# Row norms built from accumulated sums, an earlier tile 0 at each boundary, and slope tables on GpSimd, in a two-block transformer stack on one core

## The reference

```python
def first_block(x, ...):
    for i in range(2):
        h = rms_norm(x, norm_pre[i])
        y = gmlp_mixer(h, ...) if i == 0 else dilated_attention_mixer(h, ...)
        x = x + rms_norm(y, norm_post[i])
    return x

def second_block(x, mem, ...):
    for layer in range(2):
        x = layer_norm_2(A * x + 0.5 * swiglu(x, ffn_w_gu[layer, 0], ffn_w_down[layer, 0]), ...)
        o_tok, q_mem = mla_mix(x, ...) if layer == 0 else nsa_mix(x, ..., *shared)
        o_mem = memory_attention(q_mem, mem, w_mem_kv[layer])
        mix = concatenate([o_tok, o_mem]) @ w_out[layer]
        x = layer_norm_2(A * x + mix, ...)
        x = layer_norm_2(A * x + 0.5 * swiglu(x, ffn_w_gu[layer, 1], ffn_w_down[layer, 1]), ...)
        if layer == 0:
            shared = nsa_shared_kv(x, nsa_w_kv, cmp_pos, cmp_w1, cmp_b1, cmp_w2)
    return x
```

## Time and profile before

| | us |
|---|---|
| median of 3 runs | 3189.24 (3189.17 to 3189.56) |
| the profiled execution, its own time | 3191.15 |
| its span | 3189.4 |
| TensorE busy | 3021.9 |
| VectorE busy | 1295.6 |
| ScalarE busy | 1048.1 |
| GpSimd busy | 139.1 |

### The profile page before, as it was taken

How to read it: one execution, slowest core, us unless ns; L and a number is a source line. 1 busy time by engine, 2 the same in 40 slices (tenths; PEclk the granted TensorE clock), 3 DMA queues, 4 the chain that set the end, 5 groups by cost and what they waited for, 6 DMA issues and landing times.

```text
span 3189.4 us, 36596 instructions
## 1 busy us (share of the span) xinstructions
PE 3021.9 (95%) x15462; PEld 2516.9 (79%) x15462; DVE 1295.6 (41%) x1859; ACT 1048.1 (33%) x1808; POOL 139.1 (4%) x214
## 2 busy tenths in 40 slices
PE   8999989999999899999889999899999978999998
PEld 6888878888888788887668888688888854688886
DVE  3463243333326532325654332423332558553224
ACT  3323234443444322213642222113221237522221
POOL 1000010030001000001000000100000100010000
PEclk9999999999999999999999999999999979999999
DMA  5333222232221223223112332432233410122321
GB/s 194 125 102 105 93 93 67 86 94 86 82 77 47 96 90 104 93 95 100 40 40 80 99 99 93 108 106 93 93 96 102 116 40 1 40 80 93 106 93 66
DMA packets 135010, 280.06 MB, mean 88 GB/s; under 512 B 20378, under 2 KB 33098, under 8 KB 134720
## 3 DMA queue, kind: packets, MB, share of 16 engines
q1 hardware_dynamic: 125232, 247.17, 24.1%
q0 software_dynamic: 9616, 30.57, 3.0%
HBM read 271.30 MB, written 4.25 MB: 86 GB/s over the span
## 4 chain that ended last, share of the span: by engine, by line
PE 86%; DVE 8%; ACT 2%; issue 2%; DMA 1%; POOL 1%; SPq 0%; DVEq 0%; POOLq 0%; ACTq 0%
PE bank L528 24%; PE bank L530 24%; PE bank L529 24%; PE bank L681 2%; PE bank L660 2%; PE bank L714 2%; PE bank L539 1%; PE bank L542 1%; PE bank L541 1%; PE bank L733 1%; PE bank L669 1%; PE bank L722 1%; PE bank L641 1%; DVE n_p L1623 1%; DVE x_rows L1554 1%
## 5 line engine op out<-in xcount | busy, mean ns | idle before, releaser
L1492 DVE TENSOR_TENSOR w_low<-raw,w_high 128x2048 fp32r<-128x2048 f32 (+2 forms) x221 | 499.9, 2262 | 1303.4 <-ACT w_high L1135 1297.1
L528 PE MATMUL bank<-xt_high,w_high 128*128 128x512 f32 x1984 | 779.6, 393 | 3.7 <-DVE w_low L1492 3.3
L530 PE MATMUL bank<-xt_high,w_low 128*128 128x512 f32 x1984 | 773.8, 390 | 0.0
L529 PE MATMUL bank<-xt_low,w_high 128*128 128x512 f32 x1984 | 773.2, 390 | 0.0
L1135 ACT ACTIVATE w_high<-raw 128x2048 fp32r<-128x2048 f32 (+2 forms) x221 | 417.5, 1889 | 991.1 <-PE bank L530 991.1
L528 PEld LDWEIGHTS bank<-xt_high,w_high 128*128 128x128 f32 x1984 | 372.5, 188 | 81.3 <-DVE w_low L1492 3.8
L530 PEld LDWEIGHTS bank<-xt_high,w_low 128*128 128x128 f32 x1984 | 372.4, 188 | 79.8
L529 PEld LDWEIGHTS bank<-xt_low,w_high 128*128 128x128 f32 x1984 | 372.7, 188 | 75.8
L528 PE MATMUL bank<-w_high,hidden_high 128*128 128x512 f32 x704 | 277.1, 394 | 3.1 <-DVE gate_rows L1821 3.1
L529 PE MATMUL bank<-w_low,hidden_high 128*128 128x512 f32 x704 | 275.7, 392 | 0.0
L530 PE MATMUL bank<-w_high,hidden_low 128*128 128x512 f32 x704 | 275.4, 391 | 0.0
(11 more groups left out here) (327 smaller groups left out, 3902.8 us busy)
## 6 DMA issues: line engine op xcount, KB each, us to landing
raw<-in_ffn_w_gu SPq DMA_DIRECT2D x80, 1024.0 KB, 5.1
raw<-in_ffn_w_down SPq DMA_DIRECT2D x44, 1024.0 KB, 5.0
raw<-in_b_w_in SPq DMA_DIRECT2D x40, 1024.0 KB, 5.2
raw<-in_a_w_in SPq DMA_DIRECT2D x24, 1024.0 KB, 5.2
raw<-in_a_w_out SPq DMA_DIRECT2D x8, 1024.0 KB, 5.0
raw<-in_ffn_w_gu SPq DMA_DIRECT2D x16, 512.0 KB, 4.4
raw<-in_w_out SPq DMA_DIRECT2D x5, 1024.0 KB, 5.0
raw<-in_w_mem_kv SPq DMA_DIRECT2D x4, 1024.0 KB, 5.2
```

Source lines behind the costliest of these rows:

```text
L528: pe.matmul(o, lh, rh, start=start, stop=False, skip_group_check=True)
L529: pe.matmul(o, lh, rl, start=False, stop=False, skip_group_check=True)
L530: return pe.matmul(o, ll, rh, start=False, stop=stop, skip_group_check=True)
L1492: dve.tensor_tensor(homes[n][1][:, 0:w], RAW[n % 2][:, 0:w], homes[n][0][:, 0:w].bitcast(F32), ALU.subtract).then_inc(sem["w_low_ready"], ...
```

## The change

1. The last blocks of a product ahead of a boundary: tile 0 goes through both last panels first, then tile 1. Turn 0 stands between the two blocks of tile 2, turn 1 between those of tile 3 (before: ahead of them). l02 keeps the old order of the first four blocks.
2. The last panel of the product ahead of a boundary gets a home of its own (not at l02), and the homes of a boundary are free from the fifth last panel on (the fourth last where there are four panels). Both of the next product's first panels are converted ahead of tile 0 (at l02 only the first).
3. A LayerNorm tile: VectorE reads the banks with accumulated sums, makes minus the mean in one small operation, and writes (row - mean) times the gain into x; beside that ScalarE squares the centred row with an accumulated sum. VectorE makes the mean square plus epsilon, GpSimd only the power, and VectorE scales and adds the bias. VectorE waits for GpSimd's power right behind the mean square. s1 and s2 get the same small steps on VectorE, with the power alone on GpSimd. So do s0, the v norm and the MLA norms. The written order of tiles on VectorE is begin 0, end 0, begin 1, low 0, end 1, begin 2, low 1, end 2, begin 3, end 3, low 2, low 3 (`begin` is `center` or `add` below, `end` the last scaling, `low` the low part of the turned tile), with the conversions of the two edge panels in front; ScalarE's is square 0, square 1, split 0, square 2, split 1, square 3, split 2, split 3.
4. GpSimd waits for the second kv_a panel before it issues the seven loads ahead of the roots of l02.
5. The slope tables are made by GpSimd in two operations each. Table 0 follows the nsa_a product, table 1 the read of the compressed outputs, and table i from 2 on the masks of group i-2. VectorE waits for them.
6. VectorE's attention loop: at each odd n one reciprocal of two columns, and the scalings of tasks n-3 and n-2 behind it.

```diff
+    EDGES = {"s1": ("a_out", ("b", 0, 0, "q"), (64, 72, 80, 32), (0, 8)),
+             "s2": ("b_out", ("gate", 0, 0, 0), (0, 8, 24, 32), (48, 64)),
+             "l00": (("down", 0, 0), "mla_in", (16, 44, 52, 60), (0, 8)),
+             "l01": (("w_out", 0), ("gate", 0, 1, 0), (42, 50, 58, 66), (34, 74)),
+             "l02": (("down", 0, 1), "kv_a", (0, 64, 28, 48), None),
+             "l10": (("down", 1, 0), "nsa_a", (0, 8, 48, 56), (16, 24)),
+             "l11": (("w_out", 1), ("gate", 1, 1, 0), (24, 65, 32, 73), (16, 57)),
+             "l12": (("down", 1, 1), None, None, (0, 8))}
+    LATE = ("l02",)
...
+    for s, (y, after_y, places, own) in EDGES.items():
+        free = ids[y][-3 if own is None else -5 if len(ids[y]) > 4 else -4]
+        edge = [(ids[y][-1], own)] if own else []
+        if after_y:
+            edge += [(ids[after_y][i], places[2 * i:2 * i + 2]) for i in range(2)]
...
+            freed_by[g] = free
...
-            for t, i in ((0, last - 1), (1, last - 1), (0, last), (1, last), (2, last - 1), (2, last), (3, last - 1), (3, last)):
+            order = [(0, last - 1), (0, last), (1, last - 1), (1, last)]
+            if s in LATE:
+                order[1:3] = order[2], order[1]
+            for t, i in order + [(2, last - 1), (2, last), (3, last - 1), (3, last)]:
                 if t < 2:
                     pe.wait_ge(sem["w_low_ready"], at("w_low_ready", gs[i]))
-                elif i == last - 1:
-                    turn_row(s, t - 2)
                 for kk in range(2):
                     ready(2 * i + kk)
                     ins = accumulate(gs[i], i, kk, t, False, i == last and kk == 1)
                 if i == last:
                     labels = [("acc", name, t)] + ([("panel", gs[-2]), ("panel", gs[-1])] if t == TT - 1 else [])
                     ins.then_inc(sem["product_done"], step("product_done", *labels))
+                elif t >= 2:
+                    turn_row(s, t - 2)
...
+        def square_rows(t, src, to, **more):
+            return act.activation(SPARE[1][:, :, t * P:(t + 1) * P], src.rearrange("p (k n) -> p k n", k=KD), ACT.Square,
+                                  accum_out=SS[:, to:to + 1], **more)
...
+            def measure(t):
+                if kind == "ln":
+                    act.wait_ge(sem["centered"], at("centered", (s, t)))
+                    square_rows(t, R[t % 2][:], 4 * t + 2, bias=NMEAN[:, t:t + 1]).then_inc(sem["variance"], step("variance", (s, t)))
+                else:
+                    act.wait_ge(sem["product_done"], at("product_done", ("acc", y, t)))
+                    for half in range(2):
+                        ins = act.activation(SPARE[1][:, 4 * half:4 * half + 4, t * P:(t + 1) * P],
+                                             ps[2 * t + half][:].rearrange("p (k n) -> p k n", k=4), ACT.Square,
+                                             scale=D ** -0.5,
+                                             accum_out=SS[:, 4 * t + half:4 * t + half + 1])
+                    ins.then_inc(sem["squared"], step("squared", (s, t)))
...
+        def root(col, n, scale, eps, label):
+            dve.tensor_scalar(RM[:, 0:n], col, scale, eps, ALU.mult if isinstance(scale, float) else ALU.add,
+                              ALU.add).then_inc(sem["mean_square"], step("mean_square", label))
+            dve.wait_ge(sem["rstd"], at("rstd", label))
+        def normed_rows(s, t, gain):
+            dve.wait_ge(sem["squared_x"], at("squared_x", (s, t)))
+            root(SS[:, 4 * t + 2:4 * t + 3], 1, 1.0 / D, RMS_EPS, (s, t, "x"))
+            if t >= 2:
+                dve.wait_ge(sem["turned"], at("turned", (s, t - 2)))
+            dve.scalar_tensor_tensor(out=R[t % 2][:], in0=X[:, t, :], scalar=RS[:, 0:1], in1=gain,
+                                     op0=ALU.mult, op1=ALU.mult).then_inc(sem["rows_done"], step("rows_done", (s, t)))
...
+            def center(t):
+                r = R[t % 2]
+                dve.wait_ge(sem["product_done"], at("product_done", ("acc", y, t)))
+                for half in range(2):
+                    c = slice(512 * half, 512 * half + 512)
+                    ins = dve.scalar_tensor_tensor(out=r[:, c], in0=ps[2 * t + half][:], scalar=coef, in1=X[:, t, c],
+                                                   op0=ALU.mult, op1=ALU.add, accum_out=SS[:, 4 * t + half:4 * t + half + 1])
+                link(ins)
+                ins = dve.tensor_scalar(NMEAN[:, t:t + 1], SS[:, 4 * t:4 * t + 1], SS[:, 4 * t + 1:4 * t + 2], -1.0 / D,
+                                        ALU.add, ALU.mult)
+                ins.then_inc(sem["centered"], step("centered", (s, t)))
+                dve.wait_ge(sem["centered"], at("centered", (s, t)))
+                link(dve.scalar_tensor_tensor(out=X[:, t, :], in0=r[:], scalar=NMEAN[:, t:t + 1], in1=GB[0][:],
+                                              op0=ALU.add, op1=ALU.mult))
+            def add(t):
+                dve.wait_ge(sem["squared"], at("squared", (s, t)))
+                root(SS[:, 4 * t:4 * t + 1], 1, SS[:, 4 * t + 1:4 * t + 2], RMS_EPS, (s, t))
+                r = SPARE[0][:, :, t * P:(t + 1) * P]
+                for half in range(2):
+                    ins = dve.scalar_tensor_tensor(out=r[:, 4 * half:4 * half + 4, :],
+                                                   in0=ps[2 * t + half][:].rearrange("p (k n) -> p k n", k=4),
+                                                   scalar=RS[:, 0:1],
+                                                   in1=GB[0][:, 512 * half:512 * half + 512].rearrange("p (k n) -> p k n", k=4),
+                                                   op0=ALU.mult, op1=ALU.mult)
+                link(ins)
+                x = X[:, t, :].rearrange("p (k n) -> p k n", k=KD)
+                ins = dve.tensor_tensor(x, x, r, ALU.add)
+                name = "rows_done" if kind == "post" else "x_added"
+                ins.then_inc(sem[name], step(name, (s, t)))
...
+            def end(t):
+                if kind == "ln":
+                    dve.wait_ge(sem["variance"], at("variance", (s, t)))
+                    root(SS[:, 4 * t + 2:4 * t + 3], 1, 1.0 / D, LN_EPS / ALPHA ** 2, (s, t))
+                    dve.scalar_tensor_tensor(out=X[:, t, :], in0=X[:, t, :], scalar=RS[:, 0:1], in1=GB[1][:],
...
-                        link(ins)
+                        dve.wait_ge(sem["slopes_ready"], at("slopes_ready", n // 16))
...
+                if n % 2 and 3 <= n < N + 3:
+                    dve.wait_ge(sem["exp_done"], at("exp_done", (name, n - 2)))
+                    c = (n - 3) % 8
+                    link(dve.reciprocal(RD[:, c:c + 2], DS[:, c:c + 2]))
+                    for m in (n - 3, n - 2):
+                        tk = tasks[m]
+                        rd = RD[:, m % 8:m % 8 + 1]
+                        sb = tk["view"](SBs[m % 6])
+                        if tk["finish"] is not None:
+                            ins = dve.tensor_scalar(sb, sb, rd, tk["finish"], ALU.mult, ALU.mult)
+                        else:
+                            ins = dve.tensor_scalar(sb, sb, rd, None, ALU.mult)
+                        ins.then_inc(sem["p_scaled"], step("p_scaled", (name, m)))
...
+        def root(label, n=1, at_col=0):
+            pool.wait_ge(sem["mean_square"], at("mean_square", label))
+            pool.tensor_tensor(RS[:, at_col:at_col + n], RM[:, 0:n], HALF[:, 0:n], ALU.pow).then_inc(sem["rstd"], step("rstd", label))
...
         pool.wait_ge(sem["product_done"], at("product_done", ("panel", ids["down", 0, 1][-3])))
+        first, second = ids["kv_a"]
+        pool.wait_ge(sem[f"panel_loaded{second % 2}"], at(f"panel_loaded{second % 2}", second))
         load(W1[0][:], A["cmp_w1_2"][0].rearrange("(k p) n -> p k n", p=P), "w1_loaded")
...
+        pool.wait_ge(sem["nsa_const"], at("nsa_const"))
+        for i in range(HEADS // 2):
+            if i == 0:
+                pool.wait_ge(sem["product_done"], at("product_done", ("panel", ids["nsa_a"][1])))
+            if i == 1:
+                pool.wait_ge(sem["cmp_o_read"], at("cmp_o_read", TT - 1))
+            if i >= 2:
+                pool.wait_ge(sem["masked"], at("masked", ("nsa", 16 * (i - 1) - 1)))
+            for g in range(2):
+                ab = nAB[2 * (i % 2) + g][:]
+                link(pool.tensor_scalar(ab, nDI[:], -slopes[6 * g + i] / HD_SCALE, None, ALU.mult))
+                ins = pool.tensor_tensor(ab, ab, nCM[:], ALU.add)
+            ins.then_inc(sem["slopes_ready"], step("slopes_ready", i))
+        roots("l11")
```

252 lines of the change are left out of this document (100 added, 152 removed).

## The result

The changed kernel takes 3134.26 us (median of 4 runs, 3132.61 to 3135.26), against 3189.4 for the kernel before in the same comparison (3189.17 to 3191.04). The ratio is 0.9826, with a 95% interval of 0.9808 to 0.9843: 55 us less, with 3141 forecast and 3114 to 3170 stated. The two profiled executions have spans of 3189.4 and 3132.0, 57.4 apart; their stretches are compared here.

A forecast was written before the change was run, and what follows sets the result against it. TensorE bounds the kernel, busy 95% of the span; only idle, slow-clock and tail time can be won. Boundaries and tail with 4 of attention sum to 48.1 us, off the 3189.24 median: 3141 us, range 3114 to 3170.

The forecast's parts named there:

- l02: LayerNorm boundary between products, old block order kept: net gain 4 us (-6 to 9), stretch near 35.5 us.
- s1: RMS boundary between products, stretch 35.9 us: earlier start and removed GpSimd steps gain 9.0 us (6 to 12).
- s2: RMS boundary between products: second edge panel's conversion pins tile 0 about as today; gain 2.8 us (0 to 4.8).
- s0: First rows of the program: one small step moves from GpSimd to VectorE beside long work; 0 us (-1 to 1).
- l00, l01 and l11: Three LayerNorm boundaries: row 0 ready 2 us ahead of its turn, stretches 24.5 us; gains 6.0, 6.1 and 6.0 us.
- A: Rival, chance 0.19: in attention GpSimd's slope tables hold VectorE, costing about 20 us against +2; 3160 to 3165 us.
- B: Rival, chance 0.10: boundaries close wholly (46.8 us), tail 6.9, attention gives all its freed time (15); 3121 us.
- attention: Attention part: 2.1 us from tables leaving VectorE ahead of the first mask, plus 2 (-20 to +15); 4 in all.
- l10: LayerNorm boundary into nsa_a: second edge panel lands later, gap of 1.2 us; gain 3.3 us (0 to 6.5).
- tail: After TensorE's last matmul: one 5.3 us tile instead of the rest of tile 2 and all of tile 3; 6.9 gained.
- Gap 0: TensorE's wait at turn 0 in l02: grows from 4.0 to 5 or 6 us, the root following seven load issues.
- rival C: Rival, chance 0.06: in attention the paired reciprocal makes scalings late, delaying TensorE; at 1.0 us a pair 3229 us.

The follow-up runs named there:

- edge_after_row0: Changed kernel with the second edge panel converted behind tile 0, before tile 1's end, in s2 and l10 alone: 3130.0 us, ratio 0.9809 to the kernel before.
- old_order: Changed kernel with the old order of blocks and turns on TensorE in all boundaries; homes and rows as changed: 3158.0 us, ratio 0.9899 to the kernel before.
- old_stats: Changed kernel with the old VectorE statistics in LayerNorm tiles, only the power on GpSimd: 3146.7 us, ratio 0.9864 to the kernel before.
- pair_off: Changed kernel with one reciprocal for each attention task again (176 in place of 88): 3143.0 us, ratio 0.9848 to the kernel before.
- both_off: Changed kernel with attention as before the change: one reciprocal per task, all slope tables on VectorE: 3137.3 us, ratio 0.9830 to the kernel before.
- no_homes: Changed kernel without own homes for the old products' last panels, edge homes free only from the third last panel: 3170.9 us, ratio 0.9939 to the kernel before.
- l02_no_wait: Changed kernel without GpSimd's added wait for the second kv_a panel ahead of the seven loads: 3135.4 us, ratio 0.9826 to the kernel before.
- l02_rows_first: Changed kernel, in l02 roots of tiles 0 and 1 ahead of GpSimd's loads, tile 1 ended before the second edge panel's conversion: 3128.6 us, ratio 0.9801.
- best2: Changed kernel with the edits of l02_rows_first and edge_after_row0, and table 0 alone on GpSimd: 3122.4 us, ratio 0.9783 to the kernel before.

## Why the prediction was right, and where it was off

The mechanism held: most of the gain is TensorE's idle and slow-clock time at the boundaries and the time behind its last matmul. The signs named ahead were met: stretches of 23.8, 24.4 and 24.4 in l00, l01 and l11 with no wait for rows and a clock of 1.00, l02 at 35.1 with its first power at T3+17.9, and the end 5.1 us behind the last matmul. Of the signs of A one came, VectorE operations of more than twice their time beside GpSimd, but not its other one, longer groups (21.0). Of B's 46.8 us at the boundaries 39.5 came, and 5.5 of its 15 in attention. By its terms, in us:

| term | forecast | measured |
|---|---|---|
| s1 | 9.0 | 10.4 |
| s2 | 2.8 | 3.0 |
| l00, l01, l11 | 6.0, 6.1, 6.0 | 6.7, 6.2, 6.1 |
| l02 | 4.0 | 4.4 |
| l10 | 3.3 | 2.7 |
| tail | 6.9 | 7.3 |
| attention | 4 | 5.5 |
| s0 | 0 | 2.5 |
| turns inside the edge products of l01, l10, l11 | none | 3 |

*Tile 0's start.* T3+6.2 was forecast and T3+6.9 measured; the chain took 5.1 for 5.3 (its terms as listed add to 5.2). The conversion, not the accumulation, sets the start, as said. That it also pinned s2 and l10 was forecast, and edge_after_row0 shows it. The 1.20 us step on GpSimd (L1991) was rightly put down to the VectorE product beside it: in the kernel before it takes 0.19 wherever neither such a product nor a panel's low part runs beside it.

*l02.* Gap 0 was put at 5 to 6 and is 6.05, the later one at 3 to 4 and is 2.2. The prediction took the new wait to pay by the earlier panel; without it the boundary is 34.7 us, 0.4 shorter, so the step that failed there is the wait's: none of the 4.4 is its. old_order takes 1.6 of them back and old_stats 0.6; where the rest comes from is not shown.

*s1.* I read the 9.9 of the earlier trace rows as s1's longest wait. It is the start of the program; s1's was 6.28. The term was worked out from the stretch's length, 35.9, and so came near all the same.

*Attention.* The sum, 4, was near (1.8 from the first to the last NSA mask, 1.6 over the MLA masks, 2.1 ahead of the first); its parts were not argued right. I held the tables' price at GpSimd for the open question and the reciprocals for a small sure gain with a risk (rival C). A table takes 9.2 us of GpSimd where I had 3.8 to 7.8, and still the five cost 2.0 with shared reciprocals; rival A had 20. I had let a table hold VectorE for all of its time or none of it; in the traces its sums hold VectorE's scalings until they end, and GpSimd's scalings mostly do not. The ledger had a slip too, which entered no term: five tables and the 40 reciprocals of their groups free 10.5 and 6.3 us of VectorE, 16.8, where I wrote 13.8, and tables of 5.8 that hold it throughout would then cost 12, not 20. What I had missed is that the two edits depend on each other: of the 9 us that pair_off lost, 7.4 lie in the NSA tasks and 2.2 in the MLA tasks, which have no tables (the difference fell to the clock elsewhere), and with the tables on VectorE the NSA part is 3.4. That the shared reciprocal makes VectorE's queue tolerant of held scalings is my reading of this; no run isolates it. Rival C's wait came (12.6 us at n_p), but in place of a longer one: with the attention of before, in both_off, TensorE waits

```profile
PE bank L732 <- ACT n_pt L1257: 18.9, 39, 1.1
```

where the changed kernel has 2.9. pair_off settles its sign.

*s0 and the rest.* The 2.5 of s0, from the start to T3 of s1, were not foreseen, and they are mostly chance: the profiled execution of the kernel before lost 1.7 us to a slow stretch of the clock at 46 us. So did those of pair_off, old_order, no_homes, l02_no_wait, l02_rows_first and best2; that of the changed kernel and the other six did not. The kernels that had it reach T3 of s1 between 0.4 us ahead of the kernel before and 0.4 behind it. The waits at the turns inside the edge products had no term, since the stretches that I took end ahead of them. The measured terms come to 57.8 against 57.4; between them the clock's low stretches fell otherwise in both directions (1.5 us lost between s1 and s2, where the programs are alike).

*The size.* The forecast, 48, was 7 us short of the medians' 55 and 9 short of the 57.4 of the profiled executions. Of the 9, 3 are the turns inside the edge products, 2.5 s0, 2.3 the boundaries' stretches, 1.5 attention and 0.4 the tail, less what the clock took elsewhere. That the error was not larger is in part luck in l02, where the term came near by another way than the one given.

## What to carry to other kernels

At a boundary count the blocks of the bound engine between the last input of the first tile and its turn, and then ask what pins that tile's start; here the new order of blocks was worth little without the homes of panels. End a stretch where the last wait of its kind ends, or the waits behind it have no term. Before an added wait goes into a queue, look at what stands behind it: one small operation behind seven load issues cost 6 us. Two edits to one queue are to be measured together and apart, since the tables on GpSimd cost 0.85 us a group with one form of the reciprocals and nothing with the other.
